# First mixers' heads projected token-major, with VectorE making one low weight part of each head tile

## The reference, cut to what matters

```
def rmsnorm(x, g):
    y = xf * lax.rsqrt(jnp.mean(xf * xf, axis=-1, keepdims=True) + EPS)
    return y.astype(x.dtype) * g

def rope(x, cos, sin):
    x1, x2 = x[..., :half], x[..., half:ROT_DIM]
    return jnp.concatenate([x1 * c - x2 * s, x2 * c + x1 * s, x[..., ROT_DIM:]], axis=-1)
```

## Time and profile before

| | us |
|---|---|
| median of 3 runs | 2680.89 (2680.55 to 2681.11) |
| the profiled execution's own time | 2681.49 |
| its span in the trace | 2679.7 |
| TensorE busy | 2655.9 |
| VectorE, ScalarE, GpSimd busy | 1557.2, 1464.9, 860.6 |
| first layer's mixer: VC's end to the first unit's scores | 210.91 to 299.57 |
| the same in the second layer | 816.71 to 905.37 |

### The profile page before, as it was taken

How to read it: one execution, slowest core, us unless ns; L and a number is a source line. 1 busy time by engine, 2 the same in 40 slices (tenths; PEclk the granted TensorE clock), 3 DMA queues, 4 the chain that set the end, 5 groups by cost and what they waited for, 6 DMA issues and landing times.

```text
span 2679.7 us, 46362 instructions
## 1 busy us (share of the span) xinstructions
PE 2655.9 (99%) x17240; PEld 2317.2 (86%) x17240; DVE 1557.2 (58%) x2457; ACT 1464.9 (55%) x2156; POOL 860.6 (32%) x453
## 2 busy tenths in 40 slices
PE   9999999999999999999999999999999999999999
PEld 8888898888888898888889999988888899999887
DVE  5543855545543855555546787455455467873554
ACT  5445665445445665445446744754464458456643
POOL 0017663000007668000007754720010087448100
PEclk9999999999999999999999999999999999999999
DMA  6655446655655446656666743466565677425664
GB/s 219 188 179 164 134 142 190 187 189 181 188 181 162 135 141 197 188 186 192 185 186 164 159 103 80 153 193 186 189 187 185 173 173 165 89 77 177 189 186 144
DMA packets 366169, 448.03 MB, mean 167 GB/s; under 512 B 34350, under 2 KB 263856, under 8 KB 365968
## 3 DMA queue, kind: packets, MB, share of 16 engines
q1 hardware_dynamic: 364496, 443.85, 56.5%
q10 hardware_dynamic: 544, 0.95, 0.1%
q0 software_dynamic: 928, 0.45, 0.1%
HBM read 444.10 MB, written 1.05 MB: 166 GB/s over the span
## 4 chain that ended last, share of the span: by engine, by line
PE 94%; ACT 3%; DVE 2%; issue 1%; DMA 0%; SPq 0%; DVEq 0%; ACTq 0%
PE PS L521 28%; PE PS L523 28%; PE PS L522 28%; PE PS L722 1%; PE PS L1120 1%; PE PS L1193 1%; PE PS L831 1%; ACT wh L549 1%; PE PS L1183 1%; PE PS L688 1%; PE PS L1060 1%; PE PS L924 1%; DVE PS L2225 0%; PE PS L883 0%; PE PS L971 0%
## 5 line engine op out<-in xcount | busy, mean ns | idle before, releaser
L549 ACT ACTIVATE wh<-ring 128x1024 fp32r<-128x1024 f32 x840 | 885.0, 1056 | 866.3 <-PE PS L521 858.5
L557 POOL TENSOR_TENSOR wl<-ring,wh 128x1024 fp32r<-128x1024 f32 (+1 forms) x332 | 793.2, 2404 | 1622.9 <-ACT wh L549 1622.2
L557 DVE TENSOR_TENSOR wl<-ring,wh 128x1024 fp32r<-128x1024 f32 x508 | 621.5, 1225 | 611.7 <-ACT wh L549 611.4
L521 PE MATMUL PS<-wh,xh 128*128 128x512 f32 x1600 | 631.3, 395 | 1.0 <-DVE xl L1903 0.9
L523 PE MATMUL PS<-wh,xl 128*128 128x512 f32 x1600 | 622.4, 389 | 0.0
L522 PE MATMUL PS<-wl,xh 128*128 128x512 f32 x1600 | 621.4, 388 | 0.0
L521 PE MATMUL PS<-xh,wh 128*128 128x256 f32 x1856 | 545.1, 294 | 0.0
L523 PE MATMUL PS<-xh,wl 128*128 128x256 f32 x1856 | 525.6, 283 | 0.0
L522 PE MATMUL PS<-xl,wh 128*128 128x256 f32 x1856 | 525.6, 283 | 0.0
L521 PEld LDWEIGHTS PS<-xh,wh 128*128 128x128 f32 x1856 | 355.7, 192 | 15.2 <-issue 7.6
L522 PEld LDWEIGHTS PS<-xl,wh 128*128 128x128 f32 x1856 | 355.9, 192 | 7.2 <-issue 7.2
(11 more groups left out here) (319 smaller groups left out, 2573.3 us busy)
## 6 DMA issues: line engine op xcount, KB each, us to landing
ring<-in_ffn_w_in_dram SPq DMA_DIRECT2D x352, 256.0 KB, 3.0
ring<-in_mix_w_in_dram SPq DMA_DIRECT2D x256, 256.0 KB, 3.7
ring<-in_w_in_dram SPq DMA_DIRECT2D x200, 256.0 KB, 3.0
ring<-in_ffn_w_gate_dram SPq DMA_DIRECT2D x176, 256.0 KB, 2.9
ring<-in_ffn_w_up_dram SPq DMA_DIRECT2D x176, 256.0 KB, 3.1
ring<-in_ffn_w_down_dram SPq DMA_DIRECT2D x176, 256.0 KB, 2.8
ring<-in_ffn_w_out_dram SPq DMA_DIRECT2D x176, 256.0 KB, 2.7
ring<-in_w_branch_dram SPq DMA_DIRECT2D x32, 256.0 KB, 2.9
```

Of the source, the lines that this page charges most:

```text
L521: first_ = mm(o, w[0], x[0], start=start, stop=False, skip_group_check=True)
L549: act_(dst, src, ACT.Copy).then_inc(hi_ready, 1)
L557: (engine or v_).tensor_tensor(dst, src, part_views(t, wh)[0], ALU.subtract).then_inc(lo[t.slot()], 1)
```

## The change

- The head tiles become token-major, like VC. Seven tiles in place of thirteen: VC (512), SA (QA, KA, VA, KI and WI in one, 456 columns), QI (512), VB (256), BB (QB and KB, 512), QC (512), KC (512), each of four parts and two PSUM banks (0 and 1, or 2 and 3, by turns). KI and KA are made once.
- The squares are summed by VectorE (`squares`), the rotation is done by VectorE in PSUM on the 16 columns of each head alone (`sines`, `rotated`), the gain of those columns being in the tables; then the norm (`normed`). `ones64` and `rot` and their products go.
- TensorE turns a finished tile with eight transposes (`turn`), called in `after` a later tile's third part; ScalarE copies the result into `heads`, with the gain of the other columns as its scale (`take`). KC's turn stands in the gate behind the first unit's scores.
- Relu of the index stays in PSUM, and `dve_index` reads it there; `rl` goes.
- VectorE makes the low part of the fourth part of SA, QI, BB, QC and KC (`last_low`); GpSimd makes the others.
- Gates use banks 2 and 3, the values' products 0 and 1. The setup makes small sine and cosine tables by token, and tables with gains, and loads the positions by token and the gains spread to all partitions.

```diff
+MIX1_TILES = [("VC", VC, 512), ("SA", QA, 456), ("QI", QI, 512), ("VB", VB, 256), ("BB", QB, 512), ("QC", QC, 512),
+              ("KC", KC, 512)]
+LAST_PARTS = {n: FFN_TILES + 4 * i + 3 for i, (n, _, _) in enumerate(MIX1_TILES[:N_PROJ]) if n[0] != "V"}
...
+            def turn(name):
+                c = TURNED.index(name)
+                if name != "QI":
+                    pe.wait_ge(tr[2].sem, tr[2].at("y." + name))
+                if name in ("SA", "QI"):
+                    pe.wait_ge(tr[1].sem, tr[1].at("cp.KI" if name == "SA" else "cp.QI"))
+                if c:
+                    pe.wait_ge(tr[1].sem, tr[1].at("hd." + TURNED[c - 1]))
+                for i in range(4):
+                    for q in range(QT):
+                        o = i % 2 * S + q * P
+                        ins = nc.tensor.transpose(bank(4 + i // 2, o, o + P), ybuf[:, c % 2, q, i * P:(i + 1) * P], ident[:])
+                ins.then_inc(tr[0].sem, tr[0].did("t." + name))
...
+            def after(name, m):
+                if (name, m) == ("QI", 2):
+                    turn("SA")
+                elif (name, m) == ("VB", 2):
+                    turn("QI")
+                elif (name, m) == ("BB", 0):
+                    index(0)
+                elif (name, m) == ("QC", 0):
+                    index(2)
+                elif (name, m) == ("QC", 2):
+                    turn("BB")
+                elif (name, m) == ("KC", 0):
+                    index(4)
+                elif (name, m) == ("KC", 2):
+                    turn("QC")
...
+            def free(name):
+                if name == "QI":
+                    pe.wait_ge(tr[1].sem, tr[1].at("cp.VC"))
+                elif name == "VB":
+                    pe.wait_ge(tr[1].sem, tr[1].at("cp.KI"))
+                    pe.wait_ge(tr[2].sem, tr[2].at("y.SA"))
+                elif name == "BB":
+                    pe.wait_ge(tr[1].sem, tr[1].at("cp.QI"))
...
 (act_mix1, SA to BB)
+            high(e, t, 2)
+            act_(vc, made("VC"), ACT.Copy).then_inc(tr[1].sem, tr[1].did("cp.VC"))
+            high(e, t, 5)
+            square("SA")
...
+            high(e, t, 1)
+            e.wait_ge(tr[2].sem, tr[2].at("r.SA"))
...
+            root("SA")
+            high(e, t, 2)
+            take("SA")
+            high(e, t, 1)
+            high(e, t, 1)
+            e.wait_ge(tr[2].sem, tr[2].at("r.QI"))
+            act_(ybuf[:, 1], made("QI"), ACT.Copy).then_inc(tr[1].sem, tr[1].did("cp.QI"))
+            high(e, t, 2)
+            take("QI")
...
 (dve_mix1)
+            last_low("SA")
+            squares("SA")
+            sines("SA")
+            rotated("SA")
+            normed("SA")
+            last_low("QI")
+            sines("QI")
+            rotated("QI")
+            last_low("BB")
+            dve_index(e, tr, 0)
+            dve_index(e, tr, 1)
+            for i, name in enumerate(("BB", "QC")):
+                for r in (2 * i, 2 * i + 1):
+                    dve_topk(e, tr, 0, r)
+                squares(name)
+                sines(name)
+                rotated(name)
+                normed(name)
+                last_low("QC" if name == "BB" else "KC")
+                dve_index(e, tr, 2 + 2 * i)
+                dve_index(e, tr, 3 + 2 * i)
+            squares("KC")
...
 (GpSimd)
-                low(e, t, T1 - 2 * FFN_TILES + 2, nc.gpsimd)
+                for k in LAST_PARTS.values():
+                    low(e, t, k - t.k, nc.gpsimd)
+                    t.k += 1
+                low(e, t, T1 - FFN_TILES + 2 - t.k, nc.gpsimd)
```

More of the change, by code:

```diff
@@ L147, in landed @@
     def landed(self):
-        more = self.thirds + (self.third_at is not None and self.k >= self.third_at)
-        return self.turn() * 32 + 16 * more
+        return self.turn() * 32
     def width(self):
-        narrow = self.third_at is not None and self.third_at <= self.k < self.third_at + SLOTS
-        return 2 * 328 if narrow else SLOT
+        return self.widths.get(self.k, SLOT)
     def loop(self, e, rounds, tiles, body):
@@ L400, in load_step @@
         def load_step(sp, t, w, name, c, n):
[L402 to L407, removed]
+            if name == "SA":
                 for m in range(4):
@@ new lines, in index @@
+            def index(j):
+                if j == 0:
+                    pe.wait_ge(tr[1].sem, tr[1].at("hd.QI"))
+                else:
+                    pe.wait_ge(tr[2].sem, tr[2].at(f"acc{j - 1}"))
+                (q, even), (_, odd) = INDEX_HEADS[j:j + 2]
+                nk = P * (q + 1)
+                for i_, pair_ in enumerate(zip(even, odd)):
+                    for p_, h in enumerate(pair_):
+                        r = slice(p_ * HD, (p_ + 1) * HD)
+                        ins = mm(bank(6 + p_, i_ * nk, (i_ + 1) * nk),
+                                 heads[r, 2 + h // 2, q * P:(q + 1) * P], heads[r, 0, 0:nk], start=True, stop=True)
+                ins.then_inc(tr[0].sem, tr[0].did(f"index{j + 1}"))
@@ new lines, in pe_mix1 @@
+            for name, _, width in MIX1_TILES[:N_PROJ]:
+                if name == "VC":
+                    for q in range(QT):
+                        for m in range(4):
+                            if q == 0:
+                                low_ready(pe, t, m)
+                            ins = values(name, width, q, m, m, (m == 0) if q == 0 else (m > 0))
+                            if (q, m) == (0, 2):
+                                pe_xt(pe, s, 1, sqt, lambda h: pe.wait_ge(xn_made, 4 * lay + 2 + 1 + h))
+                    t.k += 4
+                else:
+                    free(name)
+                    for m in range(4):
+                        low_ready(pe, t)
+                        for q in range(QT):
+                            ins = values(name, width, q, m, 0, q == 0)
+                        t.k += 1
+                        if m < 3:
+                            after(name, m)
+                ins.then_inc(tr[0].sem, tr[0].did("p." + name))
@@ L927, in pe_mix1 @@
                 if j == 0:
-                    gate(lambda: rotate("KC1"))
+                    gate(lambda: turn("KC"))
                 else:
@@ new lines, in take @@
+            def take(name):
+                e.wait_ge(tr[0].sem, tr[0].at("t." + name))
+                at = 0
+                for to, n, r in HEADS_OUT[name]:
+                    src = PS[:, 4:6, :].rearrange("p b n -> p (b n)")[:, at:at + n * S]
+                    dst = heads[:, to:to + n, :].rearrange("p b s -> p (b s)")
+                    if r is None:
+                        ins = act_(dst, src, ACT.Copy)
+                    else:
+                        ins = act_(dst, src, ACT.Identity, scale=small[:, 6 * env.lay + r:6 * env.lay + r + 1])
+                    at += n * S
+                ins.then_inc(tr[1].sem, tr[1].did("hd." + name))
@@ new lines, in act_mix1 @@
+            high(e, t, 1)
[4 more added lines that the diff above has]
+            take("QI")
+            high(e, t, 1)
+            act_(vb, made("VB")[:, :, 0:256], ACT.Copy).then_inc(tr[1].sem, tr[1].did("cp.VB"))
+            high(e, t, 2)
+            relu(0)
+            relu(1)
+            high(e, t, 2)
+            square("BB")
+            for name, before, j in (("QC", "BB", 2), ("KC", "QC", 4)):
+                high(e, t, 1)
+                root(before)
+                high(e, t, 1)
+                relu(j)
+                relu(j + 1)
+                high(e, t, 1)
+                take(before)
+                high(e, t, 1)
+                square(name)
@@ L1518, in act_mix1 @@
+            high(e, t, 1)
+            root("KC")
+            high(e, t, 1)
             g = [0]
@@ L2207, in dve_lambda @@
             step(e, pr, v_.tensor_scalar(gd[AROWS, 0, 0:LAYERS], gd[AROWS, 0, 4:4 + LAYERS], -1.0, None, ALU.mult), "ndecay")
+            e.wait_ge(pro_act.sem, pro_act.at("cos"))
+            v_.tensor_copy(cos0[:, :, 8:16], cos0[:, :, 0:8])
+            step(e, pr, v_.tensor_scalar(sin0[:, :, 8:16], sin0[:, :, 0:8], -1.0, None, ALU.mult), "tables")
+            front = qk_gains.rearrange("p (r d) -> p r d", d=HD)[:, :, 0:16].unsqueeze(2).to_broadcast([P, 6 * LAYERS, QT, 16])
+            for gained, zero in ((cosg, cos0), (sing, sin0)):
+                ins = v_.tensor_tensor(gained, front, zero.unsqueeze(1).to_broadcast([P, 6 * LAYERS, QT, 16]), ALU.mult)
+            step(e, pr, ins, "gained_tables")
+            for r in (0, HD):
+                ins = v_.memset(small[r:r + 16, 0:6 * LAYERS], 1.0)
+            step(e, pr, ins, "head_gains")
             e.wait_ge(pro_pool.sem, pro_pool.at("cmask"))
```

390 lines of the change are left out of this document (153 added, 237 removed).

## The result

The changed kernel takes 2650.59 us (median; 2650.11 to 2650.95), the kernel before 2680.74 beside it: a ratio of 0.9887, 95% interval 0.9870 to 0.9904. That is 30.1 us less; forecast were 33.4 less, 2647.5 us. Run once more on another occasion it gave 2650.31 against 2680.69.

A forecast was written before the change was run, and what follows sets the result against it. TensorE's issue intervals were taken as the bound: 80.3 us removed less 63.6 added is 16.7 a layer, 33.4 for two, so 2680.9 - 33.4 = 2647.5 us. The range was 2644 to 2659.

The forecast's parts named there:

- What bounds the kernel: From VC's end to the first unit's scores, TensorE's own issue intervals set the time; 88.66 us in both layers.
- The ledger of 16.7 us a layer: TensorE's work per layer from VC's end on: 80.3 us removed, 63.6 us added, net 16.7 us less.
- the unit stage safer than before: From the first unit's scores on: VectorE has nothing queued at the first unit's masking after the change; no gain.
- The sum: Whole kernel: 16.7 us less a layer, 33.4 us for two, giving 2647.5 us.
- The supply of low parts: Weight parts for SA to KC, orders laid out by hand: nothing late for TensorE, slacks of 0.3 to 1.5 us.
- hand-overs late: Rival, 17%: head work at QI and BB late, some 3 to 4 us a layer, 2654 to 2656, up to 2660.
- VectorE's place in line: Rival, 4%: last low parts wait behind the previous tile's heads, stopping TensorE at five places a layer; slower than before.
- Wide products bring nothing: Rival, no chance of its own: SA's products at 0.2275 us and turns at 1.0; 1.8 us a layer, 2651.
- the boundary rival: Rival, 12%: VectorE's ready low part waits for two GpSimd instructions, at SA's and QI's fourth; 1.1 us a layer, 2649.6.
- GpSimd wins the boundary twice: The same as the boundary rival, 12%: VectorE's low part waits for two GpSimd instructions; 1.1 us a layer, 2649.6.
- The start and the setup: Ahead of or beside TensorE's wait for the first weights: setup changes worth 0, at most 0.3 us either way.

The follow-up runs named there:

- the early copy: The changed kernel, with ScalarE copying KC's turned tile between its two high parts at the first index unit, ahead of the four Exp: 2648.53 us, ratio 0.9879.
- The kernel with the fourfold sines: The changed kernel, with VectorE doing the sine products of each of the five head tiles four times instead of once: 2654.41 us.

## Why the prediction was right, and where it missed

*What bounds the kernel* held. TensorE's start intervals are the time in this stretch: 16.1 us less a layer, waits none, and helpers, turns and split products each move the time by their own intervals.

*The ledger of 16.7 us a layer* was 0.57 too good. SA took 9.92 us, forecast 9.8. The rest is restarts: by their start intervals the 512-column products beside the inserted groups took 1.0 us more than 0.227 each; the forecast had 0.08 behind a turn and 0.1 behind an index group, some 0.5 for the six. That is 1.1 us in two layers.

*A hand-over that the forecast did not lay out* is its one step that failed outright. The orders were laid out by hand for the parts of the weights and for the turns up to KC, and stopped there. KC's copy was taken to be in time at unit 1's scores; the forecast even called the unit stage safer than before, from VectorE's side alone. But ScalarE's second high part is let go only by TensorE's own step behind KC's turn, the Exp follow it, and the copy comes last. The unit stage took 127.90 us before and 128.95 after: 1.16 of stall (1.28 between the starts in place of 0.12), with a turn of 0.79 in place of a rotation of 0.86. 2.1 us in two layers, and the early copy took it away.

*The sum*: 33.4 - 1.1 - 2.1 = 30.2, measured 30.1 and 30.4. By spans it is 31.2 (2679.7 to 2648.5): 32.3 from the stretches, less 2.1, and 0.1 of start; 0.7 is a wait ahead of L1193 for nothing the profile names, in the trace of the kernel before and in no other here; 0.2 is left.

*The supply of low parts* came out as laid out. Nothing is late in the stretch, in either layer. At BB's first part the slack is some 0.4 to 0.5 us, forecast 0.3: GpSimd's low part ends at 239.01 and TensorE takes it at 239.53. SA's eleven small operations took 1.7 us, not 2.5, less than even the forecast's lowest price of 0.2 each, and QI's four took 1.4, as forecast; so "hand-overs late" (17%) didn't come. The margin is thin at QI, where half a microsecond more of head work would show at BB's first part, and wider at SA, where VectorE's low part is done at 228.30 and wanted at 230.10. The kernel with the fourfold sines lost its time at just the two places named, QI and BB. *VectorE's place in line* (4%) is further off still: four times the sines cost 4 us, not the 30 of a loss.

*Wide products bring nothing* has a time, 2651, that is nearer to the measured 2650.6 than the forecast's own 2647.5, and so has the boundary rival's 2649.6; the rows decide against both. SA's products start 0.207 us apart and not 0.2275, eight transposes take 0.79 and not 1.0, and splitting the wide products costs 5.5 us.

*GpSimd wins the boundary twice* (12%) didn't come, by the timelines of GpSimd and VectorE. The first four rows are SA's third low part on GpSimd, SA's last on VectorE, and GpSimd's next three, which begin at 215.50, 218.72 and 221.08 (two rows, which share the one at 218.72); then BB's and QC's:

```profile
213.38 2.16 POOL L557 TENSOR_TENSOR wl<-ring,wh 128x912 fp32r<-128x912 f32 x1 [0.40 <-ACT wh L549]
214.18 2.32 DVE L557 TENSOR_TENSOR wl<-ring,wh 128x912 fp32r<-128x912 f32 x1 [7.61 <-ACT wh L549]
215.50 5.62 POOL L557 TENSOR_TENSOR wl<-ring,wh 128x1024 fp32r<-128x1024 f32 x2
218.72 4.76 POOL L557 TENSOR_TENSOR wl<-ring,wh 128x1024 fp32r<-128x1024 f32 x2
...
236.62 7.07 POOL L557 TENSOR_TENSOR wl<-ring,wh 128x1024 fp32r<-128x1024 f32 x3 [1.33 <-ACT wh L549]
241.81 2.97 DVE L557 TENSOR_TENSOR wl<-ring,wh 128x1024 fp32r<-128x1024 f32 x1 [7.27 <-ACT wh L549]
...
257.05 1.23 DVE L557 TENSOR_TENSOR wl<-ring,wh 128x1024 fp32r<-128x1024 f32 x1
257.37 5.53 POOL L557 TENSOR_TENSOR wl<-ring,wh 128x1024 fp32r<-128x1024 f32 x2 [4.03 <-ACT wh L549]
```

GpSimd's instruction of 912 columns ends at 215.54. VectorE, waiting since 214.18, is done at 216.50, about 1 us behind that, and GpSimd's next lasts from 215.50 to the one behind it at 218.72, 3.2 us in place of 2.4: VectorE came in at the first boundary. The one that began at 241.81 stood until the end of GpSimd's third (243.69), behind which GpSimd had nothing ready, and was done 1.1 us later. At 257.05 VectorE was first, and GpSimd's pair took 5.53 instead of the 4.76 of 218.72. In these rows whoever runs finishes its instruction, and the one that waits is next. Only the first boundary is one where GpSimd's next was ready too; the second layer has it again (GpSimd's ends at 806.27, VectorE is done at 807.23). QI's last low part had no such neighbour. The Trainium skill ("SBUF — State Buffer", Who interferes with whom) says that the two exclude each other and that issue order decides; these rows agree, and add that a busy queue of GpSimd's doesn't keep VectorE out for a second instruction.

*The start and the setup*, forecast at 0 to 0.3, can't be read from one trace: the first product moves by more from one execution to the next.

## What to carry to other kernels

When TensorE is busy for all of a stretch, a list of its instructions with their start intervals gives what a rewrite brings to a few per cent, and small float32 helpers can be most of it: of the ledger's 16.7 us a layer they were 15.5 and the width of the products 2.4; SA and the narrower VB in place of KI, KA, QA and the wide VB were 3.1, and the turns cost 4.35. Lay out by hand every reader of what the change moves, up to and past the point where the old schedule resumes. Here an engine's order mattered more than its load: a copy of 1.1 us on an engine busy for 60% of the time stalled TensorE because it was queued behind an instruction that TensorE itself had yet to release. Moving work from an engine that kept up to another that also kept up was worth nothing, and it tied the two together.

## What the runs showed that wasn't expected

The first product of a weight in the same program begins at 9.96 or 10.36 us, and over nearly the same setups between 9.62 and 11.44, so a trace's span can't carry a difference of under 1 or 2 us by itself; subtract the start. The name in a wait is the last link only: at BB's first part "GpSimd" had been idle for 2.9 us, and the cause was three engines back.
